# Splitting the FFN norm into three parts under the output projection, and taking the final norm's roots for two row tiles at a time

## The reference, cut to what matters

```python
h = h + merged @ w_out[l]                         # 1024 x 1024 by 1024 x 1024
f = rms_norm(h, norm_ffn[l]) @ w_ff_up[l]         # to 4096 columns
h = h + jnp.square(jax.nn.relu(f)) @ w_ff_down[l] # back to 1024
return rms_norm(h, norm_final)
# rms_norm: x * rsqrt(mean(x * x, -1) + 1e-6) * g
```

## Time and profile before

| what | value |
|---|---|
| median of 3 runs | 1726.64 us (1726.24 to 1730.62) |
| the profiled execution | 1740.58 us, its span 1738.9 us |
| mean granted TensorE clock over the span | 0.976 of full |
| PE busy | 1648.5 us (95%) |
| DVE busy | 898.5 us (52%) |
| ACT busy | 553.1 us (32%) |

### The profile page before, as it was taken

One profiled execution on the slowest core, in us unless ns is written; L12 is line 12 of the kernel. 1 busy time (PEld: TensorE's weight loads), 2 busy tenths in 40 slices (PEclk: granted clock), 3 DMA queues, 4 the chain that ended last, 5 costly groups with the idle time before them and its releaser, 6 DMA issues.

```text
span 1738.9 us, 26191 instructions
## 1 busy us (share of the span) xinstructions
PE 1648.5 (95%) x10627; PEld 1315.4 (76%) x10627; DVE 898.5 (52%) x1490; ACT 553.1 (32%) x979; POOL 95.0 (5%) x175
## 2 busy tenths in 40 slices
PE   3999998899999998999989979999999999999996
PEld 2985665677878887885777868888888888888885
DVE  5357875477763832567762154444444444444437
ACT  6433454244342113444221143222222222222222
POOL 0110000000010010356000000000000000000000
PEclk9996999999999999999999989999999999999998
DMA  5020001522223354003444002111111111111102
GB/s 185 1 58 1 2 1 38 133 73 70 83 70 119 97 140 154 3 4 117 145 142 160 1 25 85 49 49 48 48 48 48 48 48 48 48 48 48 37 0 109
DMA packets 122566, 114.40 MB, mean 66 GB/s; under 512 B 24303, under 2 KB 106348, under 8 KB 121836
## 3 DMA queue, kind: packets, MB, share of 16 engines
q1 hardware_dynamic: 122368, 113.10, 21.1%
q10 hardware_dynamic: 108, 0.03, 0.0%
HBM read 90.14 MB, written 21.00 MB: 64 GB/s over the span
## 4 chain that ended last, share of the span: by engine, by line
PE 87%; DVE 7%; DMA 2%; issue 1%; ACT 1%; SPq 1%; DVEq 0%; ACTq 0%
PE bank L2283 20%; PE bank L2296 19%; PE bank L1917 18%; PE bank L2259 5%; PE bank L2217 4%; PE bank L1852 3%; PE bank L1760 2%; PE bank L1881 2%; PE bank L1865 2%; PE bank L1826 2%; DMA posi<-in_positions 1%; PE bank L2018 1%; PE bank L2127 1%; PE bank L2121 1%; PE bank L1790 1%
## 5 line engine op out<-in xcount | busy, mean ns | idle before, releaser
L1705 DVE TENSOR_TENSOR hacc<-hacc,bank 128x512 f32<-128x512 f32 x240 | 163.5, 687 | 134.6 <-PE bank L2296 134.6
L2283 PE MATMUL bank<-hT_hi,up_hi 128*128 128x512 f32 x512 | 199.8, 390 | 3.2 <-DVE up_lo L1682 3.2
L2296 PE MATMUL bank<-dn_hi,f_hi 128*128 128x512 f32 x512 | 199.4, 389 | 1.4 <-DVE hacc L1727 1.4
L2283 PE MATMUL bank<-hT_hi,up_lo 128*128 128x512 f32 x512 | 199.9, 390 | 0.0
L2283 PE MATMUL bank<-hT_lo,up_hi 128*128 128x512 f32 x512 | 199.9, 390 | 0.0
L2296 PE MATMUL bank<-dn_hi,f_lo 128*128 128x512 f32 x512 | 199.2, 389 | 0.0
L2296 PE MATMUL bank<-dn_lo,f_hi 128*128 128x512 f32 x512 | 199.2, 389 | 0.0
L1917 PE MATMUL bank<-uT_hi,w_hi 128*128 128x512 f32 x480 | 191.8, 400 | 6.3 <-DVE w_lo L1369 6.3
L1158 ACT ACTIVATE frelu<-bank 128x512 f32<-128x512 f32 x64 | 38.3, 599 | 476.4 <-PE bank L2283 427.7
L1917 PE MATMUL bank<-uT_hi,w_lo 128*128 128x512 f32 x480 | 188.4, 393 | 0.0
L1917 PE MATMUL bank<-uT_lo,w_hi 128*128 128x512 f32 x480 | 188.4, 392 | 0.0
(11 more groups left out here) (343 smaller groups left out, 2741.1 us busy)
## 6 DMA issues: line engine op xcount, KB each, us to landing
up_raw<-in_w_ff_up SPq DMA_DIRECT2D x32, 512.0 KB, 5.4
dn_raw<-in_w_ff_down SPq DMA_DIRECT2D x16, 1024.0 KB, 5.0
w_raw<-in_w_in SPq DMA_DIRECT2D x30, 512.0 KB, 4.0
sgate<-gate_spill SPq DMA_DIRECT2D x16, 512.0 KB, 4.3
gate_spill<-zbuf SPq DMA_DIRECT2D x15, 512.0 KB, 2.7
xt<-in_x SPq DMA_DIRECT2D x8, 512.0 KB, 7.8
wout_raw<-in_w_out SPq DMA_DIRECT2D x8, 512.0 KB, 4.8
hacc<-in_x SPq DMA_DIRECT2D x8, 512.0 KB, 8.9
```

The source lines that it names most:

```text
L1705: nc.vector.tensor_tensor(hacc[:, n // 2, sl], hacc[:, n // 2, sl], ps[4 + n % 4][:], ALU.add).then_inc(s_da, 1)
L2283: ins = nc.tensor.matmul(ps[2 * q + h][:], st[:, q, k, :], mv_[:, k, sl], start=(k == 0 and m == 0), stop=(k == KD - 1 and m == 2))
L2296: ins = nc.tensor.matmul(ps[4 + n % 4][:], st[:, par, q, i * P:(i + 1) * P], mv_[:, par, q, sl], start=(q == 0 and m == 0), stop=(q == 1 a ...
```

## The change

The FFN norm is made in three parts, row tiles 0 to 3, 4 to 6, and 7. Part one runs on DVE and ACT while PE is at half tiles 8 and 9 of the output projection. Its eight groups of transposes stand on PE in pairs ahead of half tiles 10 to 13. Part two follows the add of half tile 13, part three the add of half tile 15. The eight groups of tokens 512 to 1023 stand on PE after the first block of the first up product (q = 0, h = 0), and the second block waits for each k step's `hT_lo` by itself. The transposes go to banks 4 to 7. `hT` takes over the place of `mg`; other tiles move to suit: `hn` has four row tiles of room, of which three lie where `dn_raw` and `frelu` come later. The first `dn_raw` load therefore waits until all transposes are done. The first up weights are split before the last adds of the output projection.

In the final norm, the gain is waited for after six adds and not ahead of them. ACT takes the root straight from the sum of squares (scale 1/D, bias eps from a column that POOL sets at the start). DVE makes the Newton step in one column operation less, for two row tiles at once (`final_roots`), and the scaling runs two row tiles behind the adds. The last row tile is squared, scaled and stored in two halves.

```diff
-        hjunk, hjunk2 = place(203, ("hjunk", [P, D], F32)) + place(135, ("hjunk2", [P, D], F32))
-        hn, = place(75, ("hn", [P, NT, D], F32))
-        hT = place(11, ("hT_hi", [P, KD, T], F32R), ("hT_lo", [P, KD, T], F32R))
-        f_hi, f_lo = place(75, ("f_hi", [P, 2, 2, T], F32R), ("f_lo", [P, 2, 2, T], F32R))
+        hn012, hn3 = place(195, ("hn012", [P, 3, D], F32)) + place(127, ("hn3", [P, D], F32))
+        hjunk, hjunk2 = place(119, ("hjunk", [P, D], F32)) + place(135, ("hjunk2", [P, D], F32))
+        hT = mg
+        f_hi, f_lo = place(11, ("f_hi", [P, 2, 2, T], F32R), ("f_lo", [P, 2, 2, T], F32R))
         up_raw, up_hi, up_lo = place(107, ("up_raw", [P, 2, KD, P], F32), ("up_hi", [P, 2, KD, P], F32R), ("up_lo", [P, 2, KD, P], F32R))
-        dn_hi, dn_lo = place(131, ("dn_hi", [P, 2, 2, D], F32R), ("dn_lo", [P, 2, 2, D], F32R))
+        dn_hi, dn_lo = place(43, ("dn_hi", [P, 2, 2, D], F32R), ("dn_lo", [P, 2, 2, D], F32R))
         dn_raw, frelu = place(195, ("dn_raw", [P, 2, D], F32), ("frelu", [P, T], F32))
-        nfin, = place(131, ("nfin", [P, D], F32))
+        nfin, = place(43, ("nfin", [P, D], F32))
...
+        def hn(i):
+
+            return hn012[:, i % 4, :] if i % 4 < 3 else hn3[:]
+
+        NORM_PARTS = ((0, 4), (4, 7), (7, 8))
...
+                sp.wait_ge(s_tr, 4 * KD)
                 sp.dma_start(dn_raw[:], dn_d[:, 0:2, :]).then_inc(s_dn, 16)
...
+                    for h in range(2 if i == NT - 1 else 1):
+                        sl = slice(h * HALF, (h + 1) * HALF) if i == NT - 1 else slice(0, D)
+                        sp.wait_ge(s_fin, i + h + 1)
+                        sp.dma_start(out_d[i][:, sl], hacc[:, i, sl]).then_inc(s_out, 16)
+                sp.wait_ge(s_out, 16 * (NT + 1))
...
+                pch(pool, nc.gpsimd.memset(small[:, 250:251], NORM_EPS))
...
+                def root_h(part):
+                    i0, i1 = NORM_PARTS[part]
+                    act.wait_ge(s_rt, 2 + 2 * part + 1)
+                    nc.scalar.activation(small[:, 16 + i0:16 + i1], small[:, 8 + i0:8 + i1], ACT.Sqrt).then_inc(s_rt, 1)
...
+                for i in range(4):
+                    square_h(i)
+                root_h(0)
+                square_h(4)
+                for n in range(4):
+                    hT_high(n)
+                square_h(5)
+                for n in range(4, KD):
+                    hT_high(n)
                 round_up(0, 16, None)
+                square_h(6)
+                root_h(1)
+                square_h(7)
+                root_h(2)
+                for n in range(KD, 2 * KD):
+                    hT_high(n)
+                act.wait_ge(s_ss, 2 * NT)
...
-                    act.wait_ge(s_da, 2 * NT * (NG - 1) + 2 * i + 2)
-                    act.wait_ge(s_ss, NT + NT + i)
-                    nc.scalar.activation(hjunk2[:], hacc[:, i, :], ACT.Square, accum_out=small[:, 32 + i:33 + i]).then_inc(s_ss, 1)
-                    act.wait_ge(s_rt, 2 + 3 + 2 * i)
-                    nc.scalar.activation(small[:, 48 + i:49 + i], small[:, 40 + i:41 + i], ACT.Sqrt).then_inc(s_rt, 1)
+                def final_square(i, h0, h1):
+
+                    n, sl = i + h0, slice(h0 * HALF, h1 * HALF)
+                    act.wait_ge(s_da, 2 * NT * (NG - 1) + 2 * i + h1)
+                    act.wait_ge(s_ss, NT + NT + n)
+                    nc.scalar.activation(hjunk2[:, sl], hacc[:, i, sl], ACT.Square, accum_out=small[:, 32 + n:33 + n]).then_inc(s_ss, 1)
+
+                def final_root(i):
+                    nc.scalar.activation(small[:, 72 + i:73 + i], small[:, 32 + i:33 + i], ACT.Sqrt, bias=small[:, 250:251],
+                                         scale=1.0 / D).then_inc(s_rt, 1)
+
+                for i in range(NT - 1):
+                    final_square(i, 0, 2)
+                    act.wait_ge(s_ss, NT + NT + i + 1)
+                    final_root(i)
+                final_square(NT - 1, 0, 1)
+                final_square(NT - 1, 1, 2)
+                act.wait_ge(s_rt, 2 + 6 + NT - 1 + 1)
+                final_root(NT - 1)
...
-                def final(i):
-
-                    dve.wait_ge(s_ss, NT + NT + i + 1)
-                    nc.vector.tensor_scalar(small[:, 40 + i:41 + i], small[:, 32 + i:33 + i], 1.0 / D, NORM_EPS, ALU.mult,
-                                            ALU.add).then_inc(s_rt, 1)
-                    dve.wait_ge(s_rt, 2 + 4 + 2 * i)
-                    inv_root(small[:, 56 + i:57 + i], small[:, 48 + i:49 + i], small[:, 40 + i:41 + i], small[:, 232:233])
-                    nc.vector.scalar_tensor_tensor(hacc[:, i, :], hacc[:, i, :], small[:, 56 + i:57 + i], nfin[:], ALU.mult,
+                def final_roots(i):
+
+                    col = lambda c: small[:, c + i:c + i + 2]
+                    if i == NT - 2:
+                        dve.wait_ge(s_ss, NT + NT + NT + 1)
+                        last = small[:, 31 + NT:32 + NT]
+                        nc.vector.tensor_tensor(last, last, small[:, 32 + NT:33 + NT], ALU.add).then_inc(s_rt, 1)
+                        dve.wait_ge(s_rt, 2 + 6 + NT)
+                    else:
+                        dve.wait_ge(s_ss, NT + NT + i + 2)
+                    dch(dve, nc.vector.tensor_scalar(col(64), col(32), -0.5 / D, -0.5 * NORM_EPS, ALU.mult, ALU.add))
+                    dve.wait_ge(s_rt, 2 + 6 + i + (3 if i == NT - 2 else 2))
+                    dch(dve, nc.vector.reciprocal(col(88), col(72)))
+                    dch(dve, nc.vector.tensor_tensor(col(96), col(88), col(88), ALU.mult))
+                    dch(dve, nc.vector.tensor_tensor(col(96), col(96), col(64), ALU.mult))
+                    nc.vector.scalar_tensor_tensor(col(56), col(96), 1.5, col(88), ALU.add, ALU.mult).then_inc(s_fir, 1)
+
+                def final(i, h0, h1):
+                    sl = slice(h0 * HALF, h1 * HALF)
+                    dve.wait_ge(s_fir, i // 2 + 1)
+                    nc.vector.scalar_tensor_tensor(hacc[:, i, sl], hacc[:, i, sl], small[:, 56 + i:57 + i], nfin[:, sl], ALU.mult,
...
+                def norm_h(part):
+                    i0, i1 = NORM_PARTS[part]
+                    dve.wait_ge(s_ss, NT + i1)
+                    nc.vector.tensor_scalar(small[:, 8 + i0:8 + i1], small[:, i0:i1], 1.0 / D, NORM_EPS, ALU.mult, ALU.add).then_inc(s_rt, 1)
+                    dve.wait_ge(s_rt, 2 + 2 * part + 2)
+                    inv_root(small[:, 24 + i0:24 + i1], small[:, 16 + i0:16 + i1], small[:, 8 + i0:8 + i1], small[:, 232 + i0:232 + i1])
+                    if part == 1:
+                        dve.wait_ge(s_tr, 3 * KD)
+                    for i in range(i0, i1):
+                        dve.wait_ge(s_h, 2 * i + 2)
+                        nc.vector.tensor_scalar(hn(i), hacc[:, i, :], small[:, 24 + i:25 + i], None, ALU.mult).then_inc(s_xn, 1)
...
+                for n in range(8):
+                    add_h(n)
+                norm_h(0)
+                add_h(8)
+                for j in range(4):
+                    add_h(9 + j)
+                    hT_low(2 * j)
+                    hT_low(2 * j + 1)
                 rest_up(0, 1)
+                add_h(13)
+                norm_h(1)
+                add_h(14)
+                add_h(15)
+                norm_h(2)
+                for n in range(KD, 2 * KD):
+                    hT_low(n)
...
-                dve.wait_ge(s_nf, 16)
-                for i in range(NT):
-                    for h in range(2):
-                        n = 2 * i + h
-                        sl = slice(h * HALF, (h + 1) * HALF)
-                        dve.wait_ge(s_dm, 2 * NT * (NG - 1) + n + 1)
-                        nc.vector.tensor_tensor(hacc[:, i, sl], hacc[:, i, sl], ps[4 + n % 4][:], ALU.add).then_inc(s_da, 1)
-                    if i:
-                        final(i - 1)
-                final(NT - 1)
+                for n in range(2 * NT):
+                    i, h = n // 2, n % 2
+                    sl = slice(h * HALF, (h + 1) * HALF)
+                    dve.wait_ge(s_dm, 2 * NT * (NG - 1) + n + 1)
+                    nc.vector.tensor_tensor(hacc[:, i, sl], hacc[:, i, sl], ps[4 + n % 4][:], ALU.add).then_inc(s_da, 1)
+                    if i >= 2 and h == 1:
+                        if i == 2:
+                            dve.wait_ge(s_nf, 16)
+                        if i % 2 == 0:
+                            final_roots(i - 2)
+                        final(i - 2, 0, 2)
+                final_roots(NT - 2)
+                final(NT - 2, 0, 2)
+                for h in range(2):
+                    final(NT - 1, h, h + 1)
...
+                def transpose_h(n):
+                    g, k = n // KD, n % KD
+                    if k == 0:
+                        pe.wait_ge(s_xn, NT + 4 * (g + 1))
+                    if n >= 4:
+                        pe.wait_ge(s_lo, 2 * KD + n - 3)
+                    for j in range(4):
```

(50 more changed lines are left out.)

5 lines of the change are left out of this document (1 added, 4 removed).

## The result

The changed kernel ran at 1712.61 us (median of 4 runs, 1707.02 to 1720.45), the kernel before beside it at 1728.63 (4 runs): ratio 0.9886, 95% interval 0.9851 to 0.9921. In a second comparison, in alternation with the kernel before, the ratio was 0.9901 (0.9874 to 0.9927). It is faster, by 1.0 to 1.1%. The medians alone, divided, would give a little less: 0.9907 (16.0 us) and 0.9915 (1715.58 against 1730.29, 14.7 us). So the gain in time is known to a few us only. The forecast was 1707.6 us, a ratio of 0.9890.

What follows compares the result with a forecast made beforehand. PE held 87% of the chain, with DVE the bound at the kernel's end. The FFN norm's 13.9 us and the final norm's 5.1 sum to 19.0, taking 1726.64 to 1707.6 us, range 1703 to 1713.

Steps and rivals of the forecast that it cites:

- The likeliest case: Whole kernel: the forecast as worked out, 19.0 us gained, time 1707.6 us; chance 72%.
- The norm parts: Output projection's end to second up block: time above the products falls from 22.8 to 8.9 us, 13.9 us gained.
- the spare 1.3 us: Norm part three takes 4.1 us under the first up block's 5.44 us on PE, leaving 1.3 us.
- The eight groups among the products: Part one's transposes, paid on PE within the output projection: 8 x 0.53 = 4.2 us.
- The eight groups behind the first block: Transposes on PE after the first up block, paced by `hT_lo`: 4.7 us, bounds 4.2 and 8.5.
- The end: Final norm: last scaling 5.3 us earlier, tail 3.3 instead of 3.1 us; gain 5.1 us, between 4.3 and 6.
- Costed at nothing: The later `dn_raw` load has 2.5 us spare and costs nothing; POOL's memset and moved tiles at most 0.1 us.
- The rival of the late load: `dn_raw` takes 10 us instead of 5.0, at most 3 us reach PE, time 1710.6 us; chance 5%.
- The clock did not fall at the transposes: Denies the rival that PE's clock falls at the transposes: price 3.6 us, time 1711.2 us; chance 12%.
- the low clock stays: Transposes mixed into the output projection start 30.65 us at half speed: 15.3 us lost, time 1722.9, no change; chance 4%.
- slower: Half clock from half tile 10 to the first up product's end: 63 us of work doubles, 1771 us; chance 2%.
- the end stays as it is: Stores queue or the last half's square comes late: final part gives 2 instead of 5.1 us, 1710.7; chance 5%.

## Why the prediction was right

The likeliest case came, in its steps and in its sum: 19.0 us forecast, 19.7 in the stretches that the change touches (14.6 + 5.1), 20.2 in the profiled span. The absolute time was partly luck. The range took the spread of the kernel before from three runs, 4.4 us, and in one later comparison 20 runs of the kernel before spread over 16.7 us (1724.42 to 1741.07). The second median of the changed kernel, 1715.58, lies outside the 1703 to 1713, as the kernel before was slower there too. The ratio holds, the range in us was too narrow.

*The norm parts, 13.9 forecast, 14.6 measured.* The covers held: nothing waited for `hn`, neither at half tile 10 nor at the second block, and the spare 1.3 us were 1.2. The eight groups among the products cost 3.6 us instead of 4.2: two groups stand together, and the turn to the next product is paid once a pair, 0.79 us from the first transpose to the next matmul and 0.1 in slower steps behind it, where I had charged it for each group. The eight groups behind the first block took 4.55 us instead of 4.7. Moving the parts and the split of the up weights early gave 9.4 us, laying the last part under a product 5.2. That 1.5 to 1.7 us of the gain were a granted clock that no longer fell was shown by the early split of the up weights.

*The end, 5.1 forecast, 5.1 measured.* The last scaling ended 5.1 us earlier and not 5.3, as DVE's sum from the sixth add was 20.7 us and not 20.5; and the tail stayed at 3.1 where I had allowed 3.3 for stores that queue. Two errors of 0.2 us cancel. The sentence on the Trainium skill, DMA: Bandwidth & Descriptors, Anatomy of one DMA, came nearer with its 3.0 (that section describes transfers issued by GpSimd; these come from SP). That DVE is the bound from the sixth add on was shown by twenty added steps, all paid (3.8 us), and by three taken away (0.6).

*Costed at nothing.* The wait for `nfin` brought nothing, shown. The down weights' load has room: another 11 us of delay cost 5.1 us of standing, and 2.2 more by the clock that fell behind it. The rival of the late load had a smaller delay in mind, 5 us, for at most 3 us; by the room that the run showed (2.5 us ahead of ACT and 3.5 behind it) such a delay would have cost nothing, an estimate.

*The rivals.* The clock did not fall at the transposes, neither in pairs among the products nor in their own 4.55 us. The Trainium skill, TensorE: Matmul & The Clock Gate, PE-mode transpose, would have had it fall; the rows at 1.00 speak against it for this shape. Around the change, in the kernel before and in the runs above, the low level came behind PE standing idle for 3.20, 4.35, 5.09 and 6.2 us, and not behind 1.98 or 0.79. That isn't the whole story of the kernel: the long stretch at 0.50 with PE nearly always busy is there after the change too (0.56 from 130 to 165 us), and no run explains it. Nothing like it followed the transposes among the products: from 965 to 1006 us the changed kernel ran at 1.00, so *the low clock stays* and *slower* did not come. Nor did *the end stays as it is*, with 5.1 us instead of 2.

## What to carry to other kernels

A norm between two products costs little once it is cut so that only the last row tile hangs on the last product, and that one is laid under the first block of the next product which needs none of it; count the chain from add to scaled row (here 4.1 us) against the block (5.44). On an engine that sets the end by the sum of its work, one small instruction for two columns costs what it costs for one (0.16 us busy here), so pair them. Before handing work to POOL, look at what DVE reads meanwhile: a 0.16 us step was held until POOL's instruction ended, and a 128x1024 scaling for the whole of it.

## What had not been expected of the hardware

- DVE and POOL held each other up. A 128x2 step on DVE took 0.66 to 0.88 us beside a POOL multiplication of 128x1024, a 128x1024 scaling 3.47 instead of 1.28, and that multiplication itself 3.39 or 2.39 us. Adds with one input in PSUM were not slowed.
- The same fall of the clock had different prices: 0.7 us behind 4.35 us of idleness with transposes next, 1.7 us behind 3.20 and 2.2 us behind 5.09 with products next.
- The spread of runs goes with the clock. Four runs of the changed kernel took 1720.45, 1712.90, 1712.32 and 1707.02 us at mean granted clocks of 0.978, 0.982, 0.981 and 0.990. In the profiles, the output projection ended between 994.8 and 1007.3 us, though the code ahead of it is the same or nearly so. Why the low stretches ahead of it differ from run to run stays open; it is why effects under some 5 us were read from stretches.
